# Output and group projections of a two-layer decoder step: one 496-column matmul for the high and low input of 248 tokens, joined by VectorE

## The reference

```python
def pool_mlstm_layer(...):                       # layer 0
    h = rmsnorm(x, norm_g)
    proj = jnp.einsum('btd,de->bte', h, w_in)    # 2048 x 7176
    ...                                          # pooling mixer and mLSTM, each gated
    y = jnp.einsum('bte,ed->btd', jnp.concatenate([y_pool, y_m], axis=-1), w_out)   # 2048 x 2048
    return x + y.astype(x.dtype), ...

def nsa_layer(...):                              # layer 1
    h = rmsnorm(x, norm_g)
    proj = jnp.einsum('btd,de->bte', h, w_in)    # 2048 x 7216
    q, kv_c, kv_s, kv_w, gts, z = split_cols(proj, ...)
    q_rot = rope(q, q_pos)
    ...                                          # compressed, selected and window attention, gated
    y = jnp.einsum('bte,ed->btd', o * silu(z), w_out)                               # 2048 x 2048
    return x + y, ...
```

## Time and profile before

| | us |
|---|---|
| median of 3 runs (lowest, highest) | 2290.66 (2286.09, 2293.81) |
| the profiled execution | 2283.63 |
| its span | 2281.9 |
| TensorE busy in it | 2152.8 |
| VectorE busy | 874.5 |
| ScalarE busy | 718.6 |
| GpSimd busy | 757.6 |

### The profile page before, as it was taken

One profiled execution on the slowest core, in us unless ns is written; L12 is line 12 of the kernel. 1 busy time (PEld: TensorE's weight loads), 2 busy tenths in 40 slices (PEclk: granted clock), 3 DMA queues, 4 the chain that ended last, 5 costly groups with the idle time before them and its releaser, 6 DMA issues.

```text
span 2281.9 us, 43898 instructions
## 1 busy us (share of the span) xinstructions
PE 2152.8 (94%) x17957; PEld 2042.5 (90%) x17957; DVE 874.5 (38%) x1820; ACT 718.6 (31%) x998; POOL 757.6 (33%) x588
## 2 busy tenths in 40 slices
PE   3899969999999989999999999999999999999995
PEld 3899969999999989999988998899889998889995
DVE  6412203315033342115346632664346533663114
ACT  4322113324233342224224422342224322353221
POOL 1244422442434333444431243114331333113440
PEclk7999989999999999999999999999999999999998
DMA  6223354645637423546544345343634344324431
GB/s 224 82 79 80 107 159 130 171 139 125 203 94 208 130 81 98 149 114 209 144 107 130 85 126 139 85 134 94 164 100 116 94 131 119 109 78 117 115 101 77
DMA packets 453109, 282.11 MB, mean 124 GB/s; under 512 B 17112, under 2 KB 445720, under 8 KB 450611
## 3 DMA queue, kind: packets, MB, share of 16 engines
q1 hardware_dynamic: 452939, 279.71, 43.6%
HBM read 250.86 MB, written 45.99 MB: 130 GB/s over the span
## 4 chain that ended last, share of the span: by engine, by line
PE 45%; issue 32%; POOL 15%; DVE 6%; ACT 1%; POOLq 0%; DVEq 0%; ACTq 0%
PE ps L366 33%; POOL w_lo L344 15%; PE ps L1087 3%; PE ps L1182 2%; PE ps L1159 2%; PE ps L1186 1%; PE ps L986 1%; PE ps L1121 1%; PE ps L1011 1%; DVE scratch L1799 1%; PE ps L1190 1%; DVE scratch L1788 1%; DVE xy L1944 1%; DVE scratch L1790 0%; PE ps L997 0%
## 5 line engine op out<-in xcount | busy, mean ns | idle before, releaser
L344 POOL TENSOR_TENSOR w_lo<-w_raw,w_hi 128x512 fp32r<-128x512 f32 x584 | 757.4, 1328 | 1473.1 <-ACT w_hi L328 1144.3
L366 PE MATMUL ps<-h_hi,w_hi 128*128 128x260 f32 x4672 | 973.4, 290 | 50.4 <-POOL w_lo L344 25.1
L366 PE MATMUL ps<-h_hi,w_lo 128*128 128x260 f32 x4672 | 943.7, 284 | 0.0
L366 PE MATMUL ps<-h_lo,w_hi 128*128 128x260 f32 x4672 | 942.2, 283 | 0.0
L366 PEld LDWEIGHTS ps<-h_hi,w_hi 128*128 128x128 f32 x4672 | 727.4, 190 | 76.9 <-issue 34.5
L366 PEld LDWEIGHTS ps<-h_hi,w_lo 128*128 128x128 f32 x4672 | 722.6, 189 | 0.0
L366 PEld LDWEIGHTS ps<-h_lo,w_hi 128*128 128x128 f32 x4672 | 721.9, 189 | 0.0
L328 ACT ACTIVATE w_hi<-w_raw 128x2048 fp32r<-128x2048 f32 x134 | 256.7, 1916 | 120.2 <-PE ps L366 79.8
L473 DVE TENSOR_TENSOR xy<-ps,x_res 128x520 f32 (+1 forms) x32 | 22.4, 700 | 269.1 <-PE ps L366 268.7
L1386 ACT ACTIVATE scratch<-ps,scratch 128x128 f32<-128x128 f32 (+3 forms) x128 | 66.3, 523 | 133.5 <-DVE scratch L1827 133.0
L501 ACT ACTIVATE scratch<-xy 128x520 f32 (+1 forms) x32 | 20.4, 639 | 278.9 <-DVE xy L473 278.9
(11 more groups left out here) (326 smaller groups left out, 1800.6 us busy)
## 6 DMA issues: line engine op xcount, KB each, us to landing
w_raw<-in_w_in SPq DMA_DIRECT2D x114, 1024.0 KB, 5.7
w_raw<-in_w_out SPq DMA_DIRECT2D x32, 1024.0 KB, 6.1
scratch<-in_cache_kv_sel SPq DMA_DIRECT2D x256, 64.0 KB, 1.9
scratch<-in_cache_kv_win SPq DMA_DIRECT2D x128, 128.0 KB, 2.5
scratch<-in_cache_kv_cmp SPq DMA_DIRECT2D x256, 64.0 KB, 2.0
out_kvw_s<-in_cache_kv_win SPq DMA_DIRECT2D x24, 512.0 KB, 6.6
x_scratch<-xy SPq DMA_DIRECT2D x2, 4160.0 KB, 14.7
x_res<-x_scratch SPq DMA_DIRECT2D x32, 260.0 KB, 6.3
```

What stands on the lines that cost most here:

```text
L344: ins = nc.gpsimd.tensor_tensor(WL[:, t.p, k:k + 4], WR[:, t.p, k:k + 4], WH[:, t.p, k:k + 4].bitcast(F32), ALU.subtract)
L366: mm = nc.tensor.matmul(PS[:, bank + c, 0:HALF], lhsT=w[:, t.p, k, :], rhs=h[:, k, c * HALF:(c + 1) * HALF], start=(k == 0 and x == 0), st ...
```

## The change

The two input buffers become one, `H2` with the low part first (`HL`) and the high part behind (`HH`), so that one access can name both. Tiles of the two output projections and of the head groups are *joint*: in each slice one matmul of 496 columns runs the high weights over the low and the high input of tokens 0 to 247, into columns 0 to 247 and 248 to 495 of the tile's first bank. The 272 remaining tokens go to the second bank, high weights over high input, then over low input. The low weights run over the high input of the 248 and of the 272 tokens. That is five matmuls a slice. When the tile is done, VectorE adds the two parts of the first bank (`join`) and writes the 248 sums in front of the 272 others, so that the 520 tokens lie side by side across the two banks. Every reader of a joint tile comes after the join: ScalarE's swapped copies wait for it by `a_rot`, which now counts twice per rotated tile.

All other tiles keep six matmuls a slice, of 256 and 264 columns in place of 260, in another order (both products of the first part, both of the second, then the low weights), and their 520 results lie side by side too. The readers name 520 elements in a row where they named two halves.

```diff
+FRONT, JOINT = 256, 248
@@ Tile
+        self.joint = base in (O0_BASE, A_BASE, O1_BASE)
@@ buffers
-        with nc.sbuf_tensor("h_hi", [P, KT, TA], F32R) as HH, nc.sbuf_tensor("h_lo", [P, KT, TA], F32R) as HL:
+        with nc.sbuf_tensor("h_parts", [P, 2, KT, TA], F32R) as H2:
             pass
+        HL, HH = H2[:, 0], H2[:, 1]
@@ project
-                for x, (w, h) in enumerate(((WH, HH), (WH, HL), (WL, HH))):
-                    for c in range(2):
-                        mm = nc.tensor.matmul(PS[:, bank + c, 0:HALF], lhsT=w[:, t.p, k, :],
-                                              rhs=h[:, k, c * HALF:(c + 1) * HALF],
-                                              start=(k == 0 and x == 0), stop=(k == KT - 1 and x == 2))
+                wh, wl = WH[:, t.p, k, :], WL[:, t.p, k, :]
+                first, last = k == 0, k == KT - 1
+                if t.joint:
+                    cut = JOINT
+                    front, back = PS[:, bank, 0:JOINT], PS[:, bank + 1, 512 - TA + JOINT:512]
+                    mul(PS[:, bank, 0:2 * JOINT], lhsT=wh, rhs=H2[:, :, k, 0:JOINT], start=first, stop=False)
+                else:
+                    cut = FRONT
+                    front, back = PS[:, bank, FRONT:512], PS[:, bank + 1, 0:TA - FRONT]
+                    mul(front, lhsT=wh, rhs=HH[:, k, 0:FRONT], start=first, stop=False)
+                    mul(front, lhsT=wh, rhs=HL[:, k, 0:FRONT], start=False, stop=False)
+                mul(back, lhsT=wh, rhs=HH[:, k, cut:TA], start=first, stop=False)
+                mul(back, lhsT=wh, rhs=HL[:, k, cut:TA], start=False, stop=False)
+                mul(front, lhsT=wl, rhs=HH[:, k, 0:cut], start=False, stop=last)
+                mm = mul(back, lhsT=wl, rhs=HH[:, k, cut:TA], start=False, stop=last)
@@ readers
+        def whole(bank, joint, q=slice(0, P)):
+            at = bank * 512 + (1024 - TA if joint else FRONT)
+            return PF[q, at:at + TA]
+        def join(bank):
+            return nc.vector.tensor_reduce(whole(bank, True)[:, 0:JOINT],
+                                           PS[:, bank, 0:2 * JOINT].rearrange("p (a n) -> p n a", n=JOINT), AX, ALU.add)
@@ output projections, VectorE
                 dve.wait_ge(S["proj_done"], t.n + 1)
+                own.step(join(2 * t.p))
@@ head groups, ScalarE
-                        if r:
-                            act.wait_ge(S["a_rot"], 6 * g + r)
+                        act.wait_ge(S["a_rot"], 12 * g + (2 * r + 1))
@@ head groups, VectorE: scaled tiles, rotated tiles, gate tiles
                         dve.wait_ge(S["proj_done"], t.n + 1)
+                        step(join(2 * t.p))
...
+                        dve.wait_ge(S["proj_done"], t.n + 1)
+                        join(2 * t.p).then_inc(S["a_rot"], 1); own.done("a_rot")
                         dve.wait_ge(S["a_sw"], 6 * g + (r + 1))
...
                             dve.wait_ge(S["proj_done"], t.n + 1)
+                            step(join(2))
```

More of the change, by code:

```diff
@@ L346, in split_lo @@
             ins.then_inc(S["w_split"], 1)
+        mul = nc.tensor.matmul
         def project(pe, t, h_need=None, part=(0, KT), bank=None, between=None, tell=False):
@@ L378, in ps2 @@
         def ps2(t, q=slice(0, P)):
-            return PS[q, 2 * t.p:2 * t.p + 2, 0:HALF]
+            return whole(2 * t.p, t.joint, q)
+        def whole(bank, joint, q=slice(0, P)):
[4 more added lines that the diff above has]
+                                           PS[:, bank, 0:2 * JOINT].rearrange("p (a n) -> p n a", n=JOINT), AX, ALU.add)
         def ps_pair(bank, q=slice(0, P)):
@@ L480, in out_dve @@
             own.step(nc.vector.memset(RS[:], 0.0))
-            with own.turns(7, {"sq_sum": 2}) as i:
+            with own.turns(7, {"dve_step": 2, "sq_sum": 2}) as i:
                 for j in range(2):
@@ L1231, in _ @@
             act.wait_ge(S["npt_ready"], 1)
-            A(halves(S0b["zt"][:, 0]), ps2(Tile(G0_BASE, 0)), ACT.Copy).then_inc(proj_read[0], 1); act.wait_ge(proj_read[0], 1)
+            A(S0b["zt"][:, 0], ps2(Tile(G0_BASE, 0)), ACT.Copy).then_inc(proj_read[0], 1); act.wait_ge(proj_read[0], 1)
             split_hi(act, own, Tile(P_BASE, 1))
@@ L1304, in _ @@
                 act.wait_ge(S["proj_done"], t.n + 1)
-                A(halves(S0["kT"][:, 0]), ps2(t), ACT.Silu).then_inc(proj_read[t.p], 1); act.wait_ge(proj_read[t.p], t.m + 1)
+                A(S0["kT"][:, 0], ps2(t), ACT.Silu).then_inc(proj_read[t.p], 1); act.wait_ge(proj_read[t.p], t.m + 1)
                 split_hi(act, own, t.ahead(2))
@@ L1372, in _ @@
                         r = {0: 0, 1: 1, 2: 2, 3: 3, 6: 4, 8: 5}[j]
-                        if r:
-                            act.wait_ge(S["a_rot"], 6 * g + r)
-                        A(halves(RS[0:64]), ps2(t, slice(64, 128)), ACT.Copy)
-                        A(halves(RS[64:128]), ps2(t, slice(0, 64)), ACT.Copy).then_inc(S["a_sw"], 1); own.done("a_sw")
+                        act.wait_ge(S["a_rot"], 12 * g + (2 * r + 1))
+                        A(RS[0:64], ps2(t, slice(64, 128)), ACT.Copy)
+                        A(RS[64:128], ps2(t, slice(0, 64)), ACT.Copy).then_inc(S["a_sw"], 1); own.done("a_sw")
                     split_hi(act, own, t.ahead(2))
@@ L1680, in _ @@
             dve.wait_ge(S["proj_done"], t.n + 1)
-            TT(halves(XR[0:48, 0]), ps2(t, slice(0, 48)), halves(r1[0:48]), ALU.mult).then_inc(proj_read[t.p], 1)
+            TT(XR[0:48, 0], ps2(t, slice(0, 48)), r1[0:48], ALU.mult).then_inc(proj_read[t.p], 1)
             TT(cosT, cosT, r1, ALU.mult)
@@ L1908, in _ @@
                             dve.wait_ge(S["proj_done"], t.n + 1)
+                            step(join(2))
                             dve.wait_ge(S["a_rowT"], 6 * g + 6)
-                            TT(halves(XR[:, jj % 2]), PS[:, 2:4, 0:HALF], halves(r1), ALU.mult).then_inc(proj_read[t.p], 1)
+                            TT(XR[:, jj % 2], whole(2, True), r1, ALU.mult).then_inc(proj_read[t.p], 1)
                             dve.wait_ge(proj_read[t.p], t.m + 1)
```

19 lines of the change are left out of this document (10 added, 9 removed).

## The result

The kernel after takes **2310.48 us** (median of 5 runs, 2307.18 to 2312.14) beside 2288.45 (5 runs, 2282.63 to 2293.81): ratio **1.0094 [1.0074, 1.0113]**, 21.5 us slower by the ratio. The forecast was 2289.0, the range ended at 2307. Its profiled execution has a span of 2310.4 us, against 2281.9, which is 28.5 us more; so some 6 to 7 us of what the two profiles show belong to these two executions and not to the change.

A forecast was written before the change was run, and what follows sets the result against it. The prediction took TensorE, busy 94% of the span, to bound the kernel. With 15.2 us saved there and 13.5 us added by VectorE's joins, the median 2290.66 less 1.7 gave 2289.0 us, range 2262 to 2307.

The forecast's parts named there:

- I take 12.0 ns per removed matmul: TensorE, joint tiles: each matmul removed saves a fixed 12.0 ns of starting a stream at the full clock.
- 15.2 us saved: TensorE's total gain: 1264 slices that count, at 12.0 ns each.
- Rival 1: The 12 ns go with columns, 3 ns fixed or none: saves 3.8 us or nothing, 2300.4 to 2304.2 us; chance 0.28.
- in tiles 5 and 6 ... 1.2 us are left after the join: Row transposes at k = 4: the key sum ended 1.9 us earlier, so the join is covered and costs nothing.
- All four have no slack, so each grows by 0.71: Waits after tiles 3, 6 and 8 and in tile 9, per group, grow by the join: 11.4 us in all.
- the ends: Ends of first output projection, last group and last tile: each waits 0.71 us longer, 2.1 us in all.
- rival 2: The weight load sets the pace: 31.5 ns saved per slice, 39.8 us in all, 2264.4 us; chance 0.14.
- The join's row: VectorE's join, reading 496 PSUM values per partition and writing 248, takes 0.67 us.
- rival 4: VectorE's join is dearer, at twice the price: about 2306 us; chance 0.05.
- Rival 3: A 248-column projection matmul falls to the plain rate, 210 ns: 120 us more, near 2409 us; chance 0.05.

The follow-up runs named there:

- e5: Kernel after with the row transposes of tiles 5 to 7 placed after slice 6 in place of slice 4: ratio 1.0020 to the kernel before.
- e6: Kernel after with GpSimd's split of the low weights as 8 instructions of half the length in place of 4: ratio 1.0032 to the kernel before.
- e3: Kernel after with no joint tile and no join, six matmuls of 256 and 264 columns everywhere: ratio 1.0016 to the kernel before.
- e4: Kernel before with the two high-weight, low-input matmuls cut from 260 to 208 columns: 2248.35 us beside 2284.55, one run.
- e10: Kernel before with GpSimd's split in 8 instructions in every tile, row transposes where they were: 2279.92 us, ratio 0.9975.
- e8: Kernel before with row transposes after slice 6 and GpSimd's split in 8 from the head groups on: 2274.28 us, ratio 0.9944.

## Why the prediction was wrong

**The step "I take 12.0 ns per removed matmul".** Between full slices it measured 2.5 to 4 ns a slice: a tile takes 11.53 us before, 11.49 after in the first output projection and 11.47 in the second, some 0.05 us or 3.1 ns a slice on the average. The 12.0 ns that a matmul paid beyond 260 / 2.4 are 2.6 ns fixed and the rest in the columns: 0.45 ns each at the full clock, where the clock alone gives 0.417. "15.2 us saved" should have read 1264 x 3.1 = 3.9. Rival 1 had this right, with a price of 3 ns, though its 2300.4 to 2304.2 us still lie under what was measured, since its joins were as cheap as mine. Its counterargument was the reading of the earlier trace rows, that columns cost nothing extra at 1.2 GHz. It doesn't weigh: at 1.2 GHz a column comes every 0.83 ns, far above 0.45, so a limit on how fast columns are fed can't be seen there. That it is such a limit is argued; the line through six widths is measured. The Trainium skill's figure (page "TensorE: Matmul & The Clock Gate", section "Back-to-back issue gap") has the fixed part, 2.5 ns, within 0.1; its sum gives 209 ns at 496 columns, an estimate, where the trace has 226. I had put it aside because its sum failed at 260 columns; its fixed part alone was the number needed.

**The step "in tiles 5 and 6 ... 1.2 us are left after the join".** The slack of 1.9 us was right, the join's 0.71 too, and the wait came all the same: the join moved two small operations of 0.17 us each into GpSimd's split, where they take 1.15 and 1.20. I had costed an operation that is moved at its old duration. For L1002 alone that is 10.0 us more in place of the 2.8 that I had for tile 7; e5 takes it away.

**"All four have no slack, so each grows by 0.71".** Asked one by one: L1039 grew by 3.5 us in four (0.88 each), L1057 by 3.6 (0.90), by the join and a larger share of the same collision (e6: 4.2 falls to 0.2, 7.3 to 0.9). L1123 fell from 4.0 to 2.1 us in place of growing, and L1098, which I had left alone, from 4.5 to 2.2. Two things make this. First, VectorE's copy between tile 9's join and L1895; here it is in the second group before, and in the first and the second group after:

```profile
1444.32 1.16 DVE L1777 COPY scratch<-x_res 128x8 f32<-128x8 f32 x1
```
```profile
1210.05 0.17 DVE L1805 COPY scratch<-x_res 128x8 f32<-128x8 f32 x1
...
1463.88 0.46 DVE L1805 COPY scratch<-x_res 128x8 f32<-128x8 f32 x1
```

Before, it stood until GpSimd's instruction was over. Behind the join it starts 0.72 us later and ends with the same instruction: the join is paid out of time that VectorE stood anyway, and L1123 waits 1.03 us where L1095 waited 1.02. Second, in the first and third group the granted clock fell just ahead, TensorE ended tile 9 later, GpSimd's split began only at 1210.60, when the copy was done, and both waits are gone. It was the fall of the clock, and not the join, that took them away. Of the ends L1138 grew by 0.6, as said (0.71), L434 by 1.9, 1.2 of them at the first output projection's end.

**What no step had.** The granted clock. My rows held the same effect at the lower clock after an idle time; I used it for the pace and never asked which of the grown waits might set it off. Its part in the sum is small, though: two of the three new falls cost nothing on balance, the third makes the first tile of the second output projection 0.96 us longer, and the kernel before lost 1.4 us to a fall of its own that the kernel after hasn't.

**The sum again.** The starts of the tiles in the two profiles give it, after less before, saved columns and all:

| tiles | us |
|---|---|
| tile 4 of the four groups (L1039) | +3.5 |
| tiles 5, 6 and 7 (L1002) | +11.3 |
| tiles 9 and 10 (L1057, L1098, L1123) | +1.9 |
| the three ends: first output projection, last group, last tile | +1.5, +0.6, +1.3 |
| tile 130, behind the fall at 2087 us | +1.0 |
| tile 74, the fall at 1052 us that only the kernel before has | -1.4 |
| first three tiles of the first output projection | +0.9 |
| the 61 other tiles: the five matmuls in place of six | -2.1 |

That is +18.5 us, all that lies outside layer 0. The -2.1 us are 0.034 us a tile, or 3 us over 88; 0.05 a tile, 4.4 us, is what full slices alone would give. Against the forecast, with this 4.4, the saving was 10.8 us too high (15.2) and the cost 9.4 us too low (13.5 for 18.5 + 4.4 = 22.9), 20.2 together; the forecast's error by the times was 21.5 us. Two small slips in the working change nothing: rival 2's saving is 30.9 ns a slice by its own terms and not 31.5, and L1095 stands behind two slices of tile 10 and not four.

**What held.** The join's row (0.67 forecast, 0.683), so rival 4 falls. Rival 3 falls: 248 columns start the next in 114 ns. The shapes of the other 58 tiles cost nothing that e3's profile shows, though its times leave 1.6 to 5.7 us open. L1098's wait, where the clock didn't fall, is what it was, as I had it. The second output projection: rival 1 gave 184.3 us for its 1280 matmuls, 16 tiles x 11.47 are 183.5, I had 182.0. The range's lower part rested on rival 2 at full price, which e4 cuts down: the slice of e4 goes 3 ns a matmul under the pace of before.

## What to carry to other kernels

A price per instruction and a price per column look alike in a kernel with one width; find a second width, however remote, or run one, before an edit is sold on either. When an edit moves an operation in time, price it again at its new place: a copy of 8 elements cost 0.17 us alone and 1.20 beside GpSimd. And look for this collision early: cutting GpSimd's instructions in half gave the kernel before 13 us in its head groups (e10), and 5.7 us of the whole kernel, 12.8 with the later rows and layer 0 left as it was (e8), where the five matmuls of the joint form gave 4.4 at most. And a fall of the clock isn't a cost by itself: look at whether the waits behind it shrink.

## What the runs showed of the hardware

- Projection matmuls at the full clock: 0.45 ns a column + 2.6 ns, from 248 to 496 columns. With two of six cut to 208 columns a single start comes after 96 ns, but the six average 117 (e4, one run).
- A copy, scaling or two-input operation of VectorE from SBUF to SBUF that starts beside GpSimd's instruction is held until that is over: 16 elements take 1149 ns beside pieces of 1330, 602 beside 765, 176 alone. Copies of one element (144 ns), a reduction from SBUF (420), operations that read PSUM and operations already under way aren't held.
- The 1.2 GHz level in a stretch where TensorE was otherwise busy: it followed waits of 2.06 to 2.07 us in 3 of 3 cases, of 1.73 to 1.75 us in 5 of 8, of 0.91 to 0.93 us in none of 16. 1.7 us of clock went each time, and where VectorE's results were waited for just behind, the time of the tiles didn't grow by it.
